# Three projections of a hybrid layer: plain fp32 matmuls in place of three fp32r products of split operands

## The chip, the cores and the metric

The kernel runs on one core of a Trainium2 chip. The metric is device time in microseconds (us) for one execution. Times inside an execution are us from the start of its span; the span is the time from its first to its last instruction. The engines are TensorE (PE: matmuls and transposes; PEld: its weight loads), VectorE (DVE), ScalarE (ACT), GpSimd (POOL) and SyncE (SP), whose queue issues most DMAs.

## The reference, cut to what matters

Two sequences of 128 tokens (context and latent, `NS = 2`) go through two layers (`DEPTH = 2`), all in fp32.

```
h = rmsnorm(x, norm_g) * (1 + scale) + shift           # (128, 1024); shift, scale, gate from adaLN of the condition
z = h @ w_in                                           # split into the parts below
conv_in (2*512), conv_gate (512), ssm_in (512), ssm_gate (512), q (512), k (128), v (128), attn_gate (512), merge (3*1024)
branch A: GLU of conv_in, depthwise convolution of 31 taps, layernorm, silu
branch B: state space scan over ssm_in in two directions, gelu, GLU
branch C: attention with 8 query and 2 key heads
x = x + gate * ((sum of sigmoid(merge) * branch @ w_branch) @ w_out)
```

`ssm_in` and the two halves of `conv_in` are the first three projections here: columns 1536 to 2047 (unit `ssm`), 0 to 511 (`ca`, the value half) and 512 to 1023 (`cg`, the gate half).

## The kernel before, in words

**Order.** `order(l)` writes out by hand the stages of a layer, and every engine walks the same list `todo`, doing its own part of each stage. In layer 0 it starts: `hT` (2), `early` (2), `chunks cg`, `unit cg`, `preE 0`, `preP 1`, `unit ssm`, `unit ca`, `pack`, `preE 1`, ... `UT`, `S`, ... , `scan`. In layer 1 the same without `preE` and `preP`, which were done in layer 0, and with the second half of the last adaLN product (`adaEnd`) ahead of `cg` and its transposes (`adaT`) after it. Ahead of layer 0's list stands `preP 0`. `preP` is a chain of products and sums on POOL (L1766): for half 0 two rounds of two products and a sum over 128x512 (`tB`, `bbar`), then two rounds of two products (`tA`, `tB`) and a sum (`pre`) over 128x1024. `preE` transposes `pre` on PE and ACT copies it out (L1124). `S` reads its result, and the scan on DVE reads `S`.

**Operands.** `hT` holds the normalised and modulated activations, transposed: per token set 8 tiles of 128x128. Weights arrive as slabs of 2 k-tiles by 512 columns (512 KB), into a ring of `RAW = 4` buffers (`raw`); SP waits for the read of the slab four before (`slab_read`) and issues the next (L663).

**A plain unit** (`plain_slab`, L753) multiplies `hT` with the raw slab: 8 k-tiles by 2 token sets, each an fp32 matmul of 128x128 by 128x512 into one PSUM bank a token set. `q`, `kv`, `sg`, `gg`, `ag` are such units. In the trace one such matmul appears as two instructions. Its slab is released when PE has read it.

**A split unit** (`split_unit`) uses fp32r operands in two parts. Of each k-tile of weights (a chunk) ACT writes the high part (`high_parts`, L1082, a copy to fp32r) and DVE the low part (`low_parts`, L1342, raw minus high); of `hT` the same is made once (stage `early`: ACT L1201, DVE `tt_` L1342, into `mixed_split` and `gates_split`). PE then does hi*hi (L1028), hi*lo (L1029) and lo*hi (L1030) for each k-tile and token set. The slab is released when the low part of its second k-tile is done, not when PE has multiplied. Parts lie in three rooms (`CHUNK_ROOMS`): for the units in `EARLY` these are two halves of `qM` and a piece of `gates`, else pieces of `wide` and `utok`. `ahead` lets ACT and DVE work two chunks beyond the end of the unit in hand, but not from an early unit to a late one.

`cg` waits for the low part of `hT` (`early_lo`). Behind `ssm` its result goes to `utok`, from there by 8 DMAs to `wide` (`pack_u`), ACT packs it (`pack`, L1213) and PE transposes it (`UT`), which opens the way to `S`. `tt_` is the helper of DVE (L1342) and of POOL (L1766).

Of the kernel before, what the change touches and what calls it, by code (L numbers as in the profile page):

```python
# [41 lines left out]
F32 = mybir.dt.float32  # L42
F32R = mybir.dt.float32r
ALU = mybir.AluOpType
ACT = mybir.ActivationFunctionType
# [3 lines left out]
NS = 2  # L49
D = 1024  # L50
DT = D // P
DEPTH = 2
W = 512
# [25 lines left out]
ADA_COLS = D // 4  # L79
ADA_ROWS = P // 4  # L80
MERGE_OF = {"A": 0, "B": 1, "C": 2}
EARLY = ("cg", "ssm", "ca")
CHUNK_ROOMS = 3

LAST_COMB = ("comb", BRANCHES[-1], 1)
# [5 lines left out]
def order(l):  # L91

    def nxt(*stage):
        return [stage] if l + 1 < DEPTH else []

    def last(*stage):
        return [] if l + 1 < DEPTH else [stage]

    n = l + 1
    return ([("hT", 0), ("hT", 1), ("early", 0), ("early", 1), ("chunks", "cg")]  # L100
            + ([("adaEnd", l, 2)] if l else []) + [("unit", "cg")] + ([("adaT", l, 2)] if l else [])
            + ([("preE", 0, 0), ("preP", 0, 1)] if l == 0 else [])
            + [("unit", "ssm"), ("unit", "ca"), ("pack",)] + ([("preE", 0, 1)] if l == 0 else [])
            + [("bz", 0), ("UT",), ("S",), ("cp",), ("convT", 0), ("convT", 1), ("scan", 0, 16, ()),
               ("unit", "q"), ("unit", "kv"), ("scan", 16, NCHUNK, (0, 1)),
               ("unit", "sg"), ("K", 0), ("bz", 1), ("qkn", 0), ("qkn", 1)]
            + [("unit", "gg"), ("K", 1), ("unit", "ag"), ("Y",), ("qkT", 0), ("qkT", 1), ("att", 0)]
            + nxt("small", n) + nxt("tab", n) + nxt("ada", n, 0) + nxt("adaT", n, 0)
            + [("gelu", 0), ("gelu", 1)] + nxt("ada", n, 1) + [("geT", 0), ("geT", 1)] + nxt("adaT", n, 1)
            + last("split", 0) + last("split", 1) + [("att", 1), ("unit", "glub"), ("unit", "glua")]  # L110
            + (nxt("split", 0) + nxt("split", 1) + nxt("conv", 10, 21, None))
            + ([("ada", 0, 2)] if l == 0 else []) + nxt("cT", n) + ([("adaT", 0, 2)] if l == 0 else [])
            + nxt("preP", n, 0) + [("chunks", "meB0"), ("brT", "B", 0), ("brT", "B", 1)]
            + nxt("conv", 21, 26, "B0") + last("conv", 10, 17, "B0") + [("comb", "B", 0)]
            + [("brT", "C", 0), ("brT", "C", 1)] + nxt("conv", 26, TAPS, "B1") + last("conv", 17, 24, "B1")
            + [("comb", "B", 1)] + nxt("taps", n)
            + nxt("preE", n, 0) + nxt("preP", n, 1) + last("conv", 24, TAPS, "C0")
            + [("comb", "C", 0), ("cback", 0), ("cback", 1), ("comb", "C", 1)] + nxt("preE", n, 1)
            + [("brT", "A", 0), ("brT", "A", 1), ("comb", "A", 0), ("comb", "A", 1)]
            + [("wout", 0), ("wout", 1)] + nxt("xn", n, 0) + nxt("xn", n, 1) + nxt("ada", n, 2))  # L120
# [25 lines left out]
def split_unit(u):  # L146


    return u[:2] in ("me", "br", "wo") or u in EARLY


def side_uses(l, stage):
# [83 lines left out]
def build(nc, A, C, O):  # L236

    with ExitStack() as ctx:
# [15 lines left out]
        def sem(name):  # L254
            if name not in sems:
                sems[name] = ctx.enter_context(nc.semaphore(name))
            return sems[name]
# [81 lines left out]

        late_room = [wides[:, 0:2 * W], wides[:, 2 * W:4 * W], utoks[:, 0:2 * W]]  # L340

        early_room = [qMs[:, 0:2 * W], qMs[:, 2 * W:4 * W], gatess[:, 4 * W:6 * W]]
        hTe = [room[:, 0:2 * D].rearrange("p (s t q) -> p s t q", s=NS, t=DT) for room in (mixeds, gatess)]
        kz = [sb("kz0", [P, KV, P]), sb("kz1", [P, KV, 2 * P])]

        prob, probT = (pre[:, r, :, :, :].rearrange("p g j c -> p (g j c)").rearrange("p (b k) -> p b k", b=2)
# [63 lines left out]
                chunk_read.append((proj.full, proj.at[(l, u, NS - 1)][0] + 1))  # L410

        def chunk_parts(m):
            room = (early_room if chunks[m][1] in EARLY else late_room)[m % CHUNK_ROOMS]
            return room[:, 0:W], room[:, W:2 * W]

        def chunk_raw(m):
# [3 lines left out]
        def ahead(l, u, beside=2):  # L420

            m = max(i for i, c in enumerate(chunks) if c[:2] == (l, u)) + 1
            room = 0 if m == len(chunks) or (chunks[m][1] in EARLY) != (u in EARLY) else beside
            return m + room


# [20 lines left out]

        split_hi = sem("split_hi")
        split_lo = sem("split_lo")
        early_lo = sem("early_lo")  # L450
        consts_in = sem("consts_in")
        expo_in = sem("expo_in")
        rope_in = sem("rope_in")
# [57 lines left out]
        def ls(l, s):  # L511

            return NS * l + s + 1
# [21 lines left out]

        parts = []
        for l, stg in todo:
            if stg[0] in ("early", "split", "brT"):
                parts.append((l,) + stg)
            elif stg in (LAST_COMB, ("wout", 0)):  # L540
                parts += [(l, "mixT", s, int(stg != LAST_COMB)) for s in range(NS)]
# [176 lines left out]
        def _(pe):  # L718
# [45 lines left out]
            for l, stg in todo:  # L764
# [228 lines left out]
                    m.then_inc(side.full, 1)  # L993
                if k in ("unit", "comb", "wout") and stg[1] not in ("glub", "glua"):
                    for u, nk, n in units_of(stg):
                        if u in EARLY:
                            if u == EARLY[0]:
                                pe.wait_ge(early_lo, ls(l, NS - 1))
                            lhs = hTe
                        elif u[:2] == "br":  # L1000
                            for s in range(NS):
                                side.drained(pe, ("brT", l, u[2], s))
                            lhs = brTs[u[2]]
                        elif u[:2] == "me":
                            pe.wait_ge(split_lo, ls(l, NS - 1))
                            lhs = hTs
                        else:
                            lhs = hT
# [43 lines left out]
        def _(act):  # L1052
# [19 lines left out]
            def high_parts(upto):  # L1072

                for m in range(highs[0], upto):
                    l_, u, kt = chunks[m]
                    slab_landed(act, (l_, u, kt // KT_SLAB))
                    if u == "me" + BRANCHES[0] + "0" and kt == 0:
                        act.wait_ge(y_in, 16 * 8 * (l_ + 1))
                        act.wait_ge(gelu_pre, NS * (l_ + 1))
                    if m >= CHUNK_ROOMS:  # L1080
                        act.wait_ge(*chunk_read[m - CHUNK_ROOMS])
                    S.activation(chunk_parts(m)[0], chunk_raw(m), ACT.Copy).then_inc(chunk_hi, 1)  # L1082
                    highs[0] = m + 1

            for l, stg in todo:
# [51 lines left out]
                elif k == "hT":  # L1137
# [5 lines left out]
                        m = S.activation(hT[:, s, i, :], side.bank(key)[:, P * i:P * i + P], ACT.Identity,  # L1143
                                         bias=ada[:, l, i, s:s + 1], scale=gsc[:, l, i, s:s + 1])
                    m.then_inc(side.freed(key), 1)
                elif k == "unit" and stg[1] == "ca":
                    high_parts(ahead(l, "ca"))
                elif k == "unit" and stg[1] == "kv":
                    if l:
                        act.wait_ge(out_done, 64 * l)  # L1150
# [4 lines left out]
                        S.activation(v[:, s, :], proj.bank(key)[:, P:2 * P], ACT.Copy).then_inc(proj.freed(key), 1)  # L1155
                elif k == "unit" and stg[1] in ("ssm", "q"):
                    if stg[1] == "ssm":
                        high_parts(ahead(l, "ssm"))
                        if l:
                            act.wait_ge(gelu_done, NS * l)  # L1160
                    for s in range(NS):
# [6 lines left out]
                            src = src.rearrange("p (a h d) -> p a h d", a=2, h=4)  # L1168
                        S.activation(dst, src, ACT.Copy).then_inc(proj.freed(key), 1)
                elif k == "unit" and stg[1] in ("cg", "glub"):  # L1170
                    if stg[1] == "cg":
                        high_parts(ahead(l, "cg"))
                    for s in range(NS):
                        key = (l, stg[1], s)
                        proj.filled(act, key)
# [18 lines left out]
                    high_parts(ahead(l, "br" + unit, CHUNK_ROOMS))  # L1194
                elif k == "chunks":
                    high_parts(chunk_at[(l, stg[1], 0)] + CHUNK_ROOMS)
                elif k == "early":
                    s = stg[1]
                    side.drained(act, ("hT", l, s, 0))
                    side.drained(act, ("hT", l, s, 1))  # L1200
                    S.activation(hTe[0][:, s, :, :], hT[:, s, :, :], ACT.Copy).then_inc(split_hi, 1)  # L1201
                elif k == "split":
                    s = stg[1]
                    if s == 0:
# [125 lines left out]
        def _(dve):  # L1330
# [10 lines left out]
            def tt_(out, a, b, op=ALU.mult):  # L1341
                return V.tensor_tensor(out, a, b, op)  # L1342


            def low_parts(upto):

                for m in range(lows[0], upto):
                    hi, lo = chunk_parts(m)
                    dve.wait_ge(chunk_hi, m + 1)
                    tt_(lo, chunk_raw(m), hi.bitcast(F32), ALU.subtract).then_inc(chunk_lo, 1)  # L1350
                    lows[0] = m + 1
# [61 lines left out]
            for l, stg in todo:  # L1413
# [111 lines left out]
                                            gsc[:, l, d, s:s + 1], ada[:, l, d, s:s + 1], ALU.mult, ALU.add)  # L1525
                    m.then_inc(side.freed(key), 1)
                elif k == "unit" and stg[1] == "ca":
                    low_parts(ahead(l, "ca"))
                    for s in range(NS):
                        key, ka = (l, "cg", s), (l, "ca", s)  # L1530
                        proj.filled(dve, ka)
                        th_ready(dve, key)
                        V.scalar_tensor_tensor(y2[:, s, :], th_view(key), 1.0, proj.bank(ka)[:, :],
                                               ALU.add, ALU.mult).then_inc(proj.freed(ka), 1)
                elif k == "unit" and stg[1] in ("cg", "ssm"):
                    low_parts(ahead(l, stg[1]))
                elif k == "unit" and stg[1] == "glua":
                    for s in range(NS):
                        key = (l, "glua", s)
# [178 lines left out]
                                link(m)  # L1718
                elif k == "chunks":
                    low_parts(chunk_at[(l, stg[1], 0)] + CHUNK_ROOMS)  # L1720
                elif k == "early":
                    s = stg[1]
                    dve.wait_ge(split_hi, part_at[(l,) + stg] + 1)
                    tt_(hTe[1][:, s, :, :], hT[:, s, :, :], hTe[0][:, s, :, :].bitcast(F32),
                        ALU.subtract).then_inc(early_lo, 1)
                elif k == "split":
                    s = stg[1]
                    dve.wait_ge(split_hi, part_at[(l,) + stg] + 1)
# [172 lines left out]
```

## Time and profile before

| what | value |
|---|---|
| median of 3 runs | 833.03 us (832.92 to 834.3) |
| profiled execution | 833.01 us, span 831.2 us |
| mean granted TensorE clock | 0.902 |
| PE busy | 669.3 us, 81% |
| DVE busy | 605.6 us, 73% |
| ACT busy | 313.0 us, 38% |
| POOL busy | 173.8 us, 21% |

Busy time is the time in which an engine had at least one instruction running. Matmuls overlap one another, so their mean duration is longer than the distance from one to the next. Layer 0's three early units run from 51 to 99 us, those of layer 1 from 482 to 518 us.

### The profile page before, as it was taken

The page shows a single profiled execution, that of the slowest core. Times are in us where ns is not written, and L with a number is a line of the kernel's source. Part 1 is how long each engine was busy: PE and PEld are TensorE (multiplying, and loading weights), DVE is VectorE, ACT ScalarE, POOL GpSimd, SP SyncE. Part 2 cuts the span into 40 slices and gives each one's busy share as a digit, 9 for nine tenths or more (in the row PEclk, how much of TensorE's full clock was granted, in tenths as well). Part 3 has the DMA queues.
Part 4 walks back from the last instruction along what each step waited for, and adds up shares of the span by engine and source line. Part 5 has one row for each costly group of instructions (what it writes and reads, how often), then busy time and mean ns, then how long its engine had stood idle before and what let it go on. Part 6 is the DMA issues. An engine that isn't in the chain of part 4 may idle for free.

```text
span 831.2 us, 9693 instructions
## 1 busy us (share of the span) xinstructions
PE 669.3 (81%) x3450; PEld 466.9 (56%) x3450; DVE 605.6 (73%) x1103; ACT 313.0 (38%) x557; POOL 173.8 (21%) x121
## 2 busy tenths in 40 slices
PE   3757899980848964989999889999807689999996
PEld 1245765540723543866877567655407347777785
DVE  3388599997355699777767545999974567988664
ACT  1344541211423221544654445411114524545552
POOL 1088269102000046061000200591020000000000
PEclk9579999995876967999999989999958898999999
DMA  6953526350078462545554565354220124655651
GB/s 250 264 158 105 189 72 187 108 148 7 5 177 283 126 229 59 173 125 152 175 177 153 180 222 171 109 178 125 67 85 11 38 78 138 184 165 167 186 180 53
DMA packets 79339, 117.66 MB, mean 142 GB/s; under 512 B 27436, under 2 KB 31868, under 8 KB 79292
## 3 DMA queue, kind: packets, MB, share of 16 engines
q1 hardware_dynamic: 78460, 116.52, 46.1%
q10 hardware_dynamic: 832, 0.53, 0.3%
q8 instruction: 27, 0.44, 0.2%
q14 instruction: 20, 0.16, 0.1%
HBM read 112.51 MB, written 1.38 MB: 137 GB/s over the span
## 4 chain that ended last, share of the span: by engine, by line
PE 45%; DVE 37%; DMA 5%; POOL 4%; SPq 3%; ACT 3%; issue 2%; DVEq 0%; ACTq 0%; POOLq 0%
PE proj L1028 11%; PE proj L1030 11%; PE proj L1029 11%; DVE cvacc L1407 9%; DVE H L1342 8%; DVE qkt L1342 7%; DMA raw<-in_w_ada 4%; PE side L762 4%; PE proj L753 3%; PE side L959 2%; DVE wide_split L1342 2%; DVE H L1562 2%; SPq L611 1%; POOL tB L1766 1%; DVE qM_split L1342 1%
## 5 line engine op out<-in xcount | busy, mean ns | idle before, releaser
L753 PE MATMUL proj<-raw,hT 128*128 128x512 f32 (+1 forms) x320 | 125.1, 551 | 0.0
L1407 DVE SCALAR_TENSOR_TENSOR cvacc<-cvpad,taps,cvacc 128x256 f32<-128x256 f32 x240 | 122.9, 540 | 0.0
L1342 DVE TENSOR_TENSOR wide_split<-raw,wide_split 128x512 fp32r<-128x512 f32 x118 | 90.8, 774 | 40.1 <-ACT wide_split L1082 39.1
L1082 ACT ACTIVATE wide_split<-raw 128x512 fp32r<-128x512 f32 x118 | 74.6, 633 | 95.6 <-PE proj L1030 95.6
L753 PEld LDWEIGHTS proj<-raw,hT 128*128 128x128 f32 x320 | 60.3, 190 | 60.4 <-issue 58.4
L1342 DVE TENSOR_TENSOR H<-H,qkt 128x128 f32<-128x128 f32 x128 | 75.4, 589 | 1.2
L1028 PE MATMUL proj<-wide_split,H_split 128*128 128x512 f32 x154 | 64.7, 420 | 14.1 <-DVE wide_split L1342 13.6
L1770 POOL TENSOR_SCALAR st<-st 128x1 f32<-128x1 f32 (+1 forms) x12 | 3.9, 326 | 331.3 <-DVE st L1679 146.9
L730 PE MATMUL proj<-raw,cond 128*32 128x256 f32 x384 | 43.6, 561 | 26.7 <-DMA raw<-in_w_ada 26.6
L957 PE MATMUL side<-qM,Uz 128*64 128x64 f32 x128 | 19.8, 241 | 54.4 <-DVE HY L1663 54.4
L1030 PE MATMUL proj<-wide_split,H_split 128*128 128x512 f32 x154 | 62.3, 404 | 0.0
L1029 PE MATMUL proj<-wide_split,H_split 128*128 128x512 f32 x154 | 62.3, 404 | 0.0
L1342 DVE TENSOR_TENSOR utok_split<-raw,utok_split 128x512 fp32r<-128x512 f32 x58 | 45.4, 783 | 18.4 <-ACT utok_split L1082 17.4
L1082 ACT ACTIVATE utok_split<-raw 128x512 fp32r<-128x512 f32 x58 | 36.7, 632 | 42.9 <-PE proj L1030 42.9
L1342 DVE TENSOR_TENSOR qM_split<-raw,qM_split 128x512 fp32r<-128x512 f32 x32 | 37.0, 1167 | 19.7 <-ACT qM_split L1082 19.6
L957 PEld LDWEIGHTS side<-qM,Uz 128*64 128x64 f32 x128 | 14.2, 155 | 56.0 <-issue 56.0
L1028 PEld LDWEIGHTS proj<-wide_split,H_split 128*128 128x128 f32 x154 | 29.9, 194 | 26.9 <-DVE wide_split L1342 18.0
L730 PEld LDWEIGHTS proj<-raw,cond 128*32 128x32 f32 x384 | 10.1, 133 | 55.4 <-DMA raw<-in_w_ada 51.8
L1028 PE MATMUL proj<-qM_split,mixed_split 128*128 128x512 f32 x64 | 27.6, 432 | 15.7 <-DVE qM_split L1342 15.7
L1342 DVE TENSOR_TENSOR qkt<-H,lamI 128x128 f32<-128x128 f32 x64 | 37.3, 582 | 1.4
L1182 ACT ACTIVATE gates<-proj 128x512 f32<-128x512 f32 x12 | 7.1, 597 | 75.9 <-PE proj L753 62.6
L1766 POOL TENSOR_TENSOR tA<-cT,lamr 128x1024 f32<-128x1024 f32 (+1 forms) x12 | 19.7, 1642 | 74.4 <-PE side L863 73.6
(235 smaller groups left out, 1496.2 us busy)
## 6 DMA issues: line engine op xcount, KB each, us to landing
raw<-in_w_in SPq DMA_DIRECT2D x104, 512.0 KB, 3.7
raw<-in_w_ada SPq DMA_DIRECT2D x48, 512.0 KB, 5.2
raw<-in_w_out SPq DMA_DIRECT2D x16, 512.0 KB, 3.9
raw<-in_w_ssm_glu SPq DMA_DIRECT2D x8, 512.0 KB, 5.7
raw<-in_w_ssm_out SPq DMA_DIRECT2D x8, 512.0 KB, 3.8
raw<-in_w_attn_out SPq DMA_DIRECT2D x8, 512.0 KB, 4.0
raw<-in_w_conv_out SPq DMA_DIRECT2D x8, 512.0 KB, 4.0
raw<-in_w_in SPq DMA_DIRECT2D x8, 256.0 KB, 2.7
```

The costliest lines, as they stand in the source:

```text
L730: m = T.matmul(proj.bank(stg)[ADA_ROWS * j:ADA_ROWS * j + ADA_ROWS, 0:ADA_COLS], cond[:, kt, :], w[:, 0, ADA_COLS * j:ADA_COLS * j + ADA_C ...
L753: m = T.matmul(proj.bank((l, u, s))[:, 0:n], lhs[:, s, kt, :], w[:, i, :], start=(kt == 0), stop=last)
L762: return T.transpose(out, in_, ident[0:k, 0:k])
L957: T.matmul(o, Uz[:, g, :], M[:, :, g // 2, :], start=True, stop=False)
L959: m = T.matmul(o, HY[:, q % 2, gi, r, :, :].rearrange("p s k -> p (s k)"), CP[:, r, 1:L + 1, g, :], start=False, stop=(r == 1))
L1028: T.matmul(bank[:, :], hi, whi, start=(kt == 0), stop=False)
L1029: T.matmul(bank[:, :], hi, wlo, start=False, stop=False)
L1030: m = T.matmul(bank[:, :], lo, whi, start=False, stop=last)
L1082: S.activation(chunk_parts(m)[0], chunk_raw(m), ACT.Copy).then_inc(chunk_hi, 1)
L1342: return V.tensor_tensor(out, a, b, op)
L1407: m = V.scalar_tensor_tensor(acc, src, taps[:, t, j:j + 1], acc, ALU.mult, ALU.add)
L1766: return Q.tensor_tensor(out, a, b, op)
```

## The change

`EARLY` is gone: `cg`, `ssm` and `ca` are no longer split units. PE multiplies `hT` with the raw slabs in `plain_slab`, as it does for `q` or `gg`. The stages `early` (the split of `hT`) and `chunks cg` (the first three chunks) leave the order, and so do the calls of `high_parts` and `low_parts` in these three units, the early rooms and the semaphore `early_lo`. In place of `early_lo`, PE waits ahead of `cg` until both halves of `hT` are written for both token sets. `ahead` stops at the end of a layer, where it used to stop at the edge between early and late units. Slabs of the three units are now released by PE's reads.

```diff
@@ order
-    return ([("hT", 0), ("hT", 1), ("early", 0), ("early", 1), ("chunks", "cg")]
+    return ([("hT", 0), ("hT", 1)]
@@ split_unit
-    return u[:2] in ("me", "br", "wo") or u in EARLY
+    return u[:2] in ("me", "br", "wo")
@@ chunk_parts, ahead
-            room = (early_room if chunks[m][1] in EARLY else late_room)[m % CHUNK_ROOMS]
+            room = late_room[m % CHUNK_ROOMS]
...
-            room = 0 if m == len(chunks) or (chunks[m][1] in EARLY) != (u in EARLY) else beside
+            room = 0 if m == len(chunks) or chunks[m][0] != l else beside
@@ tensor engine
-                        if u in EARLY:
-                            if u == EARLY[0]:
-                                pe.wait_ge(early_lo, ls(l, NS - 1))
-                            lhs = hTe
-                        elif u[:2] == "br":
+                        if u == "cg":
+                            for s in range(NS):
+                                for h in range(2):
+                                    side.drained(pe, ("hT", l, s, h))
+                        if u[:2] == "br":
@@ scalar engine
-                elif k == "unit" and stg[1] == "ca":
-                    high_parts(ahead(l, "ca"))
...
-                        high_parts(ahead(l, "ssm"))
...
-                        high_parts(ahead(l, "cg"))
...
-                elif k == "early":
-                    s = stg[1]
-                    side.drained(act, ("hT", l, s, 0))
-                    side.drained(act, ("hT", l, s, 1))
-                    S.activation(hTe[0][:, s, :, :], hT[:, s, :, :], ACT.Copy).then_inc(split_hi, 1)
@@ vector engine
-                    low_parts(ahead(l, "ca"))
...
-                elif k == "unit" and stg[1] in ("cg", "ssm"):
-                    low_parts(ahead(l, stg[1]))
...
-                elif k == "early":
-                    s = stg[1]
-                    dve.wait_ge(split_hi, part_at[(l,) + stg] + 1)
-                    tt_(hTe[1][:, s, :, :], hT[:, s, :, :], hTe[0][:, s, :, :].bitcast(F32),
-                        ALU.subtract).then_inc(early_lo, 1)
```

## Rows read from the trace of the kernel before

**Rows 1.** The page's busy time, share of the span and instructions of each engine.
```profile
PE 669.3 (81%) x3450; PEld 466.9 (56%) x3450; DVE 605.6 (73%) x1103; ACT 313.0 (38%) x557; POOL 173.8 (21%) x121
```

**Rows 2.** Chain of waits, layer 0: start us, us, what.
```profile
66.16 2.72 POOL pre L1766
...
83.80 2.80 DVE qM_split L1342
...
99.38 2.43 PE side L762 x24
```

**Rows 3.** Chain of waits, layer 1.
```profile
476.40 3.77 DMA raw<-in_w_in
...
480.85 0.70 DVE qM_split L1342
...
513.98 0.23 PE proj L1028
...
517.90 0.24 PE proj L1030
```

**Rows 4.** Instructions in order, layer 0: start, us, engine, line, what [idle before <-releaser].
```profile
40.77 3.53 SPq L663 DMA_DIRECT2D raw<-in_w_in  x4
...
44.24 1.36 DVE L1524 TENSOR_SCALAR hT<-side,gsc,ada 128x128 f32<-128x128 f32 x4 [0.21 <-PE side L762]
...
51.05 0.77 PE L1028 MATMUL proj<-qM_split,mixed_split 128*128 128x512 f32 x1 [6.85 <-DVE qM_split L1342]
...
70.68 0.48 PE L1028 MATMUL proj<-gates_split,mixed_split 128*128 128x512 f32 x1
...
78.97 0.50 PE L1028 MATMUL proj<-qM_split,mixed_split 128*128 128x512 f32 x1 [1.11 <-DVE qM_split L1342]
```

**Rows 5.** Instructions in order, PE alone, layer 1: the unit `gg` and what follows it.
```profile
567.51 14.00 PE L753 MATMUL proj<-raw,hT 128*128 128x512 f32 x32
581.44 4.63 PE L876 MATMUL side<-EC,bz 128*48 128x80 f32 x64
```

**Rows 6.** DMA issues from 40.5 to 41.3 us: count, KB each, us to landing.
```profile
raw<-in_w_in SPq DMA_DIRECT2D x1, 512.0 KB, 5.4
```

**Rows 7.** Stretches, PE alone: us, busy us (instructions), granted clock, DMA share, GB/s.
```profile
51.00:53.50 2.50, 2.45 (x6) 0.50 0.03 3
...
66.00:99.30 33.30, 27.45 (x119) 1.00 0.39 121
...
481.70:487.00 5.30, 5.30 (x13) 0.50 0.67 236
...
627.20:630.80 3.60, 3.60 (x34) 0.50 0.00 0
```

**Rows 8.** Instructions in order, layer 1.
```profile
475.37 1.37 DVE L1524 TENSOR_SCALAR hT<-side,gsc,ada 128x128 f32<-128x128 f32 x4 [0.57 <-PE side L762]
...
481.69 0.76 PE L1028 MATMUL proj<-qM_split,mixed_split 128*128 128x512 f32 x1 [3.53 <-DVE qM_split L1342]
...
514.62 1.90 ACT L1213 ACTIVATE HY<-wide 64x2048 f32<-64x2048 f32 x1
...
518.06 1.14 PE L762 MATMUL side<-ident,HY 64*128 64x64 f32 x15
```

**Rows 9.** Instructions in order, POOL alone.
```profile
43.93 2.19 POOL L1766 TENSOR_TENSOR tB<-ss,tA 128x512 f32<-128x512 f32 x2 [15.83 <-DMA tA<-in_ssm_b_im]
...
61.28 2.36 POOL L1766 TENSOR_TENSOR tA<-lamr,bbar 128x1024 f32<-128x1024 f32 x1
...
71.08 2.05 POOL L1766 TENSOR_TENSOR tA<-lamr,bbar 128x1024 f32<-128x1024 f32 x1 [2.20 <-PE side L762]
...
117.35 1.93 POOL L1766 TENSOR_TENSOR tA<-cT,lamr 128x1024 f32<-128x1024 f32 x1
...
311.04 1.34 POOL L1766 TENSOR_TENSOR bbar<-tB 128x512 f32<-128x512 f32 x1
...
324.15 2.42 POOL L1766 TENSOR_TENSOR pre<-tA,tB 128x1024 f32<-128x1024 f32 x1
```

More of the change, by code:

```diff
@@ L81 @@
 MERGE_OF = {"A": 0, "B": 1, "C": 2}
-EARLY = ("cg", "ssm", "ca")
 CHUNK_ROOMS = 3
@@ L340, in build @@
         late_room = [wides[:, 0:2 * W], wides[:, 2 * W:4 * W], utoks[:, 0:2 * W]]
-        early_room = [qMs[:, 0:2 * W], qMs[:, 2 * W:4 * W], gatess[:, 4 * W:6 * W]]
-        hTe = [room[:, 0:2 * D].rearrange("p (s t q) -> p s t q", s=NS, t=DT) for room in (mixeds, gatess)]
         kz = [sb("kz0", [P, KV, P]), sb("kz1", [P, KV, 2 * P])]
@@ L449, in build @@
         split_lo = sem("split_lo")
-        early_lo = sem("early_lo")
         consts_in = sem("consts_in")
@@ L537, in build @@
         for l, stg in todo:
-            if stg[0] in ("early", "split", "brT"):
+            if stg[0] in ("split", "brT"):
                 parts.append((l,) + stg)
@@ L1170, in _ @@
                 elif k == "unit" and stg[1] in ("cg", "glub"):
-                    if stg[1] == "cg":
-                        high_parts(ahead(l, "cg"))
                     for s in range(NS):
```

## The prediction
> **What bounds the kernel now.** I read the busy shares first [rows 1]: TensorE (PE) is at 81% and VectorE (DVE) at 73%, so neither alone sets the time. Then I read the chain of waits in the two stretches that the change touches, one in each layer.
>
> In layer 0 [rows 2] the chain is not the matmuls. It runs on GpSimd (POOL) up to the last `pre` product of `preP`, which ends at 68.9, goes through the four banks of transposes of `preE` half 0, and then sits on the low parts that DVE makes of the raw slabs, up to 2.8 us each where layer 1 needs 0.70 [rows 3]. PE runs the `ssm` unit from 70.68 [rows 4], and the transposes that open the rest of the layer start at 99.38, when `ca` is through. Everything after that hangs on it in series: transposes, `S`, and the scan on DVE.
>
> In layer 1 [rows 3] nothing runs on POOL at that time. The chain waits for the first slab of `w_in` (3.77 us from 476.40, there at 480.17), passes one copy and one subtraction, and from 481.69 to the `UT` transposes at 518.06 [rows 8] it is matmul after matmul: PE is the bound, for 36.4 us. The mean of the profiled matmuls (0.40 us) is no price here, since they overlap; the distance from one to the next is: 17 steps from 513.98 to 517.90, 0.231 us each [rows 3].
>
> The time: the profiled execution took 833.01 us around a span of 831.2; the median of the runs shown is 833.03. The sum below is a difference to the execution, and carries over as it is.
>
> **What the change does to PE.** Each layer has three such units of 8 k-tiles by 2 token sets. Now each pair costs three fp32r matmuls, 3 x 0.231 = 0.69 us; a unit is 48 matmuls, 11.1 us. Afterwards it is one plain fp32 product, which the trace holds as two instructions. The later unit `gg` has that very shape: it took from 567.51 to 581.44, 13.93 us, with the clock at full rate and no gap [rows 5]. So each unit costs PE 2.8 us more where PE is what is waited for, and it is so in layer 1 throughout, in layer 0 only where DVE held it at less than that.
>
> Removed with it, per layer: 24 copies on ScalarE (ACT, 0.63 us), 24 subtractions on DVE, and the split of `hT`, two instructions on either. What of it shows in the end is worked out below by stage: in layer 1 the copy and subtraction ahead of the first matmul (1.5 us), in layer 0 what it did to POOL. The rest lies beside PE's matmuls and gives nothing. Nothing is added on any queue. Slabs are now released by PE's last read, no more by the low parts which ran ahead; a slab feeds PE for 3.5 us (13.93 / 4), three others are in hand (10.4 us), and a slab took 3.8 to 5.4 us from issue to landing [rows 3, 6], so I cost this at nothing. `gg` lives on the same release and shows no gap.
>
> **Layer 1.** PE starts when the slab is there, 480.2, in place of 481.69: 1.5 us gained (`hT` is finished before, at 476.7 [rows 8]). Then 3 x 13.93 = 41.8, and the small transposes between `cg` and `ssm`, 0.2, which is what is left of the 36.4 when 144 x 0.231 = 33.3 and the clock's 2.9 are taken off. The clock has to be added. Here the granted clock had fallen to half during the wait and stayed there until about 487.5, 5.8 us long, which lost 2.9; after the start of `cg` in layer 0 it was low for only 2.9 us, from 51.05 to 54.0, which lost 1.5 [rows 7]. PE's idle time before the new start is 2.0 us, not 3.5. I take 2.2, the middle of these, with 0 and 2.9 as bounds. The end: 480.2 + 41.8 + 0.2 + 2.2 = 524.4, against 518.06: **+6.3 us** (+4.1 to +7.0). The packing of `u`, which `UT` needs too, ended at 516.5, 1.5 us ahead of those transposes [rows 8]; it counts from the end of `ssm`, and the `ca` unit that lies over it grows by 2.8, so it does not come last.
>
> **Layer 0.** Four steps.
> First, `cg` can start when `hT` is drained (45.6) and the first slab has landed, 40.77 + 5.4 = 46.2 [rows 4, 6], in place of 51.05. With 13.9 and 1.5 to 2.9 of low clock it ends at 61.6 to 63.0. That gives nothing: PE then waits for `pre` from POOL.
> Second, POOL itself. While DVE subtracts, the two alternate: a 128x1024 product of `preP` takes 2.36, a sum 2.72 [rows 2, 9]. Where DVE was idle at its start a product took 2.05, and a sum took 2.42 beside a tap of the convolution; a 128x512 sum took 1.34 in layer 1's `preP`, and two 128x512 products 2.19 with the 0.07 between them, 1.06 each [rows 9]. After the change DVE is idle from 45.6 until `ca`. With 0.07 us between instructions: 43.93 + 2 x (1.13 + 1.13 + 1.41) + 2 x (2.12 + 2.12 + 2.49) = 64.8 in place of 68.9: **-4.1 us**. The bounds are nothing and that.
> Third, the `preE` transposes as before, 1.8 from the end of `pre` (68.88) to `ssm` (70.68) [rows 2, 4]: `ssm` starts at 66.6.
> Fourth, `ssm` and `ca`: 27.9 instead of 28.7 (70.68 to 99.38, much of it DVE's pace): -0.8. So the end is 94.5 at full clock, 4.9 earlier.
> Against it stands the clock. Before, PE waited in this stretch too, but no more than 1.1 us at a time (before 78.97), and the granted clock stayed at 1.00 [rows 4, 7]. Now PE idles 1.8 to 3.2 us ahead of the transposes. After its idle stretches of 6.85 us (before 51.05) and 3.53 us (before 481.69) the clock was low [rows 4, 8]. I take 1.5, bounds 0 and 2.9. Layer 0: **-3.4 us** (-4.9 to -2.0).
>
> The Trainium skill, page "SBUF — State Buffer", section "Who interferes with whom", says that a DVE instruction with two SBUF inputs and a GpSimd instruction that reads SBUF exclude each other for a whole instruction. By that rule all of POOL's excess (2.36 against 2.05) goes away; the rows above give the same 4.1, and without the rule the bound of nothing would weigh more.
> The skill's page "TensorE: Matmul & The Clock Gate", section "HAM oscillation — how this bites in real kernels", says that a tensor engine kept idle between bursts drops to half clock and starts each burst cold. By it the new gap in layer 0 costs a whole low spell and not my compromise of 1.5; the rival (b) prices that from rows.
>
> Sum: -3.4 + 6.3 = +2.9; 833.0 + 2.9 = **835.9 us**. Behind either stretch the work is a chain to the end of the layer, so I let both differences pass through unchanged.
>
> **Rivals.**
> (a) As forecast: 835.9, own range 834.7 to 837.4. Chance 0.50.
> (b) The clock falls at both starts and stays low for the long spell seen in layer 1: -2.0 + 7.0 = +5.0, 838.0. For it: both long waits before had that effect. Against: the gaps are shorter. 0.20.
> (c) POOL isn't faster alone, `pre` still ends at 68.9. PE has then idled some 6 us, the clock is low for certain: 27.9 + 2.9 against 28.7 gives +2.1, with +6.3 it is +8.4, 841.4. For it: I infer the alternation from durations, and in the scan stage POOL's products take 1.93 beside a busy DVE [rows 9], as if it cost POOL nothing. Against: the 2.05 of [rows 9] beside the 2.36. 0.10.
> (d) The other side. The price of layer 1 is certain, so a gain could come from the clock alone: full at both starts, -4.9 + 4.1 = -0.8, 832.2; and if the burst of `Y` matmuls, 3.6 us at half rate before [rows 7], also starts warm, 1.8 more: 830.4. It counts as faster only when more than 4.6 of the 5.5 us at stake (1.5 + 2.2 + 1.8) is saved. 0.05 for that, 0.10 for the part that ends between 832.2 and 834.
> (e) PE waits for slabs after all, since they are requested later. The nearest row is the 3.77 us of the first slab in layer 1 [rows 3]; one such wait more in each layer gives +2.9 + 7.6 = +10.5, 843.5. 0.05.
>
> A measurement of this kernel tells about 0.2%, 1.7 us, from no change: 831.4 to 834.7 counts as the same. Slower: (a), (b), (c), (e) = 0.85; same 0.10; faster 0.05. The range from 832.4 to 841.0 leaves out (c), (e) and the faster part of (d), less than 0.2.
>
> **What would show it.** In the profile after: 32 matmuls of 13.9 us in each of the six units; in layer 0 a PE start near 46, idle time near 62, `pre` done near 64.8 with products of 2.05, and the block of transposes before `UT` near 96 (99.4 before); in layer 1 a start 1.5 us earlier relative to the adaLN matmuls, and about 44 us from there to `UT`. The prediction is wrong if `pre` ends near 68.9, if the granted clock differs by more than 3 us of low spell from what I took, if slabs are waited for inside a unit, or if the differences don't reach the end.

## The result and the profile after

The changed kernel takes 836.11 us, the median of 9 runs (834.4 to 839.15), beside 832.73 for the kernel before on the same chips (9 runs, 831.33 to 834.3). The ratio is 1.0035, 95% interval 1.0022 to 1.0049, which is 2.9 us slower (1.8 to 4.1); the two medians differ by 3.4. The profiled execution took 836.93, 0.8 over the median, around a span of 835.1: 3.9 more than the 831.2 before. The lines below explain the 3.9.

The page, busy time of the engines, answering to [rows 1]:

```profile
PE 689.5 (83%) x3354; PEld 453.9 (54%) x3354; DVE 543.6 (65%) x1051; ACT 280.2 (34%) x505; POOL 168.6 (20%) x121
```

DVE is relieved of 62 us and the kernel is slower all the same: nearly all of that work lay beside something else. PE has 20 us more.

**Layer 0.** The chain of waits (start us, us, what), answering to [rows 2]:

```profile
62.00 2.35 POOL pre L1744
...
64.39 3.49 PE side L758 x16
67.89 27.61 PE proj L749 x64
95.50 2.43 PE side L758 x24
...
99.42 1.14 PE side L859 x8
```

The low parts are gone from it. Between POOL's last sum and the transposes that open the rest of the layer there are only PE's own blocks. They start at 95.50, 3.9 us earlier than before (99.38).

Instructions in order, POOL and then PE, answering to [rows 4, 9]:

```profile
43.96 2.19 POOL L1744 TENSOR_TENSOR tB<-ss,tA 128x512 f32<-128x512 f32 x2 [15.78 <-DMA tA<-in_ssm_b_im]
46.23 1.27 POOL L1744 TENSOR_TENSOR bbar<-tB 128x512 f32<-128x512 f32 x1
...
57.80 2.02 POOL L1744 TENSOR_TENSOR tA<-lamr,bbar 128x1024 f32<-128x1024 f32 x1
...
62.00 2.34 POOL L1744 TENSOR_TENSOR pre<-tA,tB 128x1024 f32<-128x1024 f32 x1
```
```profile
46.32 15.67 PE L749 MATMUL proj<-raw,hT 128*128 128x512 f32 x32 [1.95 <-DMA raw<-in_w_in]
64.39 3.49 PE L758 MATMUL side<-ident,pre 128*128 128x128 f32 x16 [2.40 <-POOL pre L1744]
67.68 27.81 PE L749 MATMUL proj<-raw,hT 128*128 128x512 f32 x64
```

POOL starts where it did. Its first two products take 2.19 us as before; from the first sum on (46.23) every instruction of its chain is shorter, and `pre` is done at 64.34, where it was 68.88. PE is through with `cg` at about 62.0, waits 2.40 us, and then takes 3.3 us (64.39 to 67.68) for the 16 transposes that took 1.8 before. The stretches, PE alone (us, busy us, granted clock), say why, and answer to [rows 7]:

```profile
62.00:64.00 2.00, 0.00 (x0) 1.00 0.36 60
64.80:67.80 3.00, 3.00 (x16) 0.50 0.10 34
68.50:95.00 26.50, 26.50 (x63) 1.00 0.48 143
...
475.50:477.50 2.00, 0.45 (x1) 1.00 1.04 397
478.00:481.00 3.00, 3.00 (x5) 0.50 0.85 307
481.50:520.00 38.50, 38.50 (x93) 1.00 0.59 172
```

The clock is still full in the idle time and at half (1.2 GHz) just when PE has work again: it falls at about 64.7 and 477.7, 0.3 and 0.6 us after PE has begun, and is back at 68.1 and 481.1. It was at half at the start of `cg` in layer 0 too, from 47.5 to 50.9, behind the wait of 1.95 us; that is why `cg` took 15.67 us there, where it takes 13.97 at full clock (in the kernel with added subtractions, below).

**Layer 1.** The chain of waits, answering to [rows 3, 8]:

```profile
472.12 1.06 PE proj L726 x8
...
473.20 3.71 DMA raw<-in_w_in
476.91 0.14 issue
477.05 15.67 PE proj L749 x32
492.71 0.22 PE side L758 x2
...
522.56 1.14 PE side L859 x8
```

From the last adaLN block to the first matmul of `S` it was 475.32 to 520.29, 44.97 us; now it is 472.12 to 522.56, 50.44. That is +5.5.

The rest: 372.7 us from the first matmul of `S` in layer 0 to the adaLN block (372.0 before), and 312.5 from `S` of layer 1 to the end (310.9). So -3.9 + 0.7 + 5.5 + 1.6 = +3.9. The two stretches that the change touches give +1.6 of it, the two whose code is the same +2.3.

### The profile page after: what moved, and what is told of

It is laid out like the page before. It is cut to its first block, busy times and chain, and to the rows that moved or that the text cites. A ratio compares the mean times of both kernels' runs of the same rounds, so it can differ in the third digit from the quotient of the medians.

```text
span 835.1 us, 9347 instructions
## 1 busy us (share of the span) xinstructions
PE 689.5 (83%) x3354; PEld 453.9 (54%) x3354; DVE 543.6 (65%) x1051; ACT 280.2 (34%) x505; POOL 168.6 (20%) x121
## 4 chain that ended last, share of the span: by engine, by line
PE 48%; DVE 35%; DMA 5%; POOL 4%; SPq 3%; ACT 2%; issue 2%; DVEq 0%; ACTq 0%; POOLq 0%
PE proj L749 11%; PE proj L1024 9%; PE proj L1025 9%; PE proj L1026 9%; DVE cvacc L1393 9%; DVE H L1328 8%; DVE qkt L1328 7%; DMA raw<-in_w_ada 4%; PE side L758 4%; PE side L955 2%; DVE wide_split L1328 2%; DVE H L1545 2%; SPq L607 1%; PE side L953 1%; DVE qk L1328 1%
## 5 line engine op out<-in xcount | busy, mean ns | idle before, releaser
L749 PE MATMUL proj<-raw,hT 128*128 128x512 f32 (+1 forms) x512 | 211.9, 574 | 4.0 <-DMA raw<-in_w_in 4.0
L749 PEld LDWEIGHTS proj<-raw,hT 128*128 128x128 f32 x512 | 97.9, 193 | 111.4 <-issue 107.1
L1393 DVE SCALAR_TENSOR_TENSOR cvacc<-cvpad,taps,cvacc 128x256 f32<-128x256 f32 x240 | 119.5, 525 | 0.0
L1328 DVE TENSOR_TENSOR H<-H,qkt 128x128 f32<-128x128 f32 x128 | 73.6, 575 | 1.2
L1518 DVE SCALAR_TENSOR_TENSOR mixed<-th,proj 128x512 f32<-128x512 f32 x4 | 2.8, 688 | 75.7 <-PE proj L749 75.7
L1024 PEld LDWEIGHTS proj<-wide_split,H_split 128*128 128x128 f32 x154 | 30.2, 196 | 27.8 <-DVE wide_split L1328 17.2
L1026 PEld LDWEIGHTS proj<-wide_split,H_split 128*128 128x128 f32 x154 | 30.3, 196 | 7.3
L1025 PEld LDWEIGHTS proj<-wide_split,H_split 128*128 128x128 f32 x154 | 30.4, 197 | 5.8
```

Source lines behind the costliest of these rows:

```text
L749: m = T.matmul(proj.bank((l, u, s))[:, 0:n], lhs[:, s, kt, :], w[:, i, :], start=(kt == 0), stop=last)
L1024: T.matmul(bank[:, :], hi, whi, start=(kt == 0), stop=False)
L1025: T.matmul(bank[:, :], hi, wlo, start=False, stop=False)
L1026: m = T.matmul(bank[:, :], lo, whi, start=False, stop=last)
L1393: m = V.scalar_tensor_tensor(acc, src, taps[:, t, j:j + 1], acc, ALU.mult, ALU.add)
```

## The experiments

Unless said otherwise each kernel was timed in 5 rounds against the kernel before. Ratios are turned into us with 833.

### Each layer by itself

`EARLY` became a list of pairs of layer and unit, so that the units of one layer are split and those of the other plain. The first list leaves layer 0 plain, the second layer 1.

```diff
-    return u[:2] in ("me", "br", "wo") or u in EARLY
+    return u[:2] in ("me", "br", "wo") or (l, u) in EARLY_AT
...
+EARLY_AT = ((1, 'cg'), (1, 'ssm'), (1, 'ca'))
...
+EARLY_AT = ((0, 'cg'), (0, 'ssm'), (0, 'ca'))
```

> Plain fp32 units in layer 0 alone; layer 1 keeps the split ones. Theory (the change is a gain in layer 0, because POOL's chain is no longer slowed by DVE, and a loss in layer 1, because PE needs 13.9 instead of 11.1 us a unit): 3 to 4 us faster than before, near 829.3, with the transposes before UT of layer 0 near 95.5 as in the profile of the change. Rival (layer 0's earlier end is lost again behind it, and the whole +3.4 stems from some common cost): within 1 us of before.

Measured: 828.73 us, ratio 0.9935 (0.9912 to 0.9959): 5.4 us faster than before (3.4 to 7.3).

> Plain fp32 units in layer 1 alone; layer 0 keeps the split ones. Theory: 5.5 to 7 us slower than before, near 839, from the start of the first unit to UT about 43.3 us in place of 36.4. Rival (both layers carry half of the +3.4): 1.5 to 2 us slower. The differences of this kernel and of the one with layer 0 alone should add up to the +3.4 of the whole change within 1 us.

Measured: 841.22 us, ratio 1.0078 (1.0053 to 1.0102): 6.5 us slower (4.4 to 8.5). In its profile the stretch from the adaLN block to `S` is 50.36 us (476.18 to 526.54), that of the change to 0.1 us. The profile of this kernel also shows how far an untouched stretch can move: with the same split units as before in layer 0, `S` of layer 0 starts at 105.38, 2.1 us later than before (103.30).

What follows: the change is a gain and a loss. Both rivals fall, no common cost and no equal halves. The sum of the two is +1.1, the whole change +2.9; they differ by 1.8, more than the 1 us that I allowed, but each of the two ratios is only known to about 2 us. By the medians (833.4 for the kernel before in these rounds) the two are -4.7 and +7.8, +3.1 in sum beside the +3.4 of the whole change, within what I allowed; the runs don't tell more exactly. In the profile of the first kernel the transposes before `UT` start at 93.64:

```profile
46.21 16.96 PE L756 MATMUL proj<-raw,hT 128*128 128x512 f32 x32 [1.89 <-DMA raw<-in_w_in]
64.33 2.00 PE L765 MATMUL side<-ident,pre 128*128 128x128 f32 x16 [1.17 <-POOL pre L1779]
66.17 27.63 PE L756 MATMUL proj<-raw,hT 128*128 128x512 f32 x64
93.64 1.94 PE L765 MATMUL side<-ident,pre 128*128 128x128 f32 x16
```

That is 1.7 earlier than in the change (95.33 in the same view), with the same work. Here `cg` took 16.96 and left PE only 1.17 us to wait, and the transposes ran at full clock. Whether executions of one kernel differ in this way isn't shown, since each has one profile.

### One unit alone

```diff
+EARLY_AT = ((0, 'cg'), (0, 'ssm'), (0, 'ca'), (1, 'cg'), (1, 'ssm'))
```

> Only the last of the three units of layer 1 (ca) as plain fp32, all else as before. Theory (13.93 - 11.1 a unit, nothing at the start): 2.8 us slower, near 835.5; the unit itself 13.9 us. Rival (the loss of layer 1 is in its first unit, the clock and the start, not in the rate): less than 1 us slower.

Measured: 837.88 us (12 runs, 833.33 to 839.13), ratio 1.0035 (1.0017 to 1.0054): 2.9 us slower (1.4 to 4.5). The medians differ by 4.5, since the 12 runs lie wide apart. The chain of waits in its layer 1:

```profile
508.48 0.23 PE proj L1038
508.71 13.75 PE proj L756 x32
```

The unit took 13.75 us where 48 split matmuls take 11.1. From the adaLN block to `S` it was 47.58 us (477.03 to 524.61), 2.6 more than before (44.97). The loss is the rate, 2.7 us a unit, as the theory had it; the rival falls.

### What slowed POOL

Twelve instructions on DVE in the changed kernel, where it is otherwise idle:

```diff
+                    if l == 0 and s == 1:
+                        for i in range(12):
+                            link(tt_(gates[:, i % 2, 0, :], x[:, 0, 0:W], x[:, 1, 0:W], ALU.subtract))
```

> The changed kernel with 12 DVE instructions added right after hT of layer 0: subtractions of two 128x512 fp32 halves of x in SBUF, into a tile that is overwritten later. They do nothing for the result and no one waits for them. Theory (two SBUF operands on DVE slow POOL): preP's 128x1024 products go back from 2.02 to about 2.36 and the sums from 2.34 to 2.7, pre ends near 68 in place of 64.3, and the kernel is 3 to 4.5 us slower than the change, near 840. Rival (POOL was slowed by ACT's copies or the loads, not by DVE): pre still ends near 64.4 and the time is that of the change, 836.1.

Measured: 840.68 us, ratio 1.0089 (1.0074 to 1.0103). Against the change, 1.0089 - 1.0035 = 0.54%, 4.5 us slower. DVE, then POOL, in order:

```profile
45.12 23.37 DVE L1328 TENSOR_TENSOR gates<-x 128x512 f32<-128x512 f32 x12
```
```profile
59.69 2.35 POOL L1747 TENSOR_TENSOR tA<-lamr,bbar 128x1024 f32<-128x1024 f32 x1
...
64.55 2.67 POOL L1747 TENSOR_TENSOR pre<-tA,tB 128x1024 f32<-128x1024 f32 x1
```

The counterpart, DVE as busy with one operand in SBUF:

```diff
+                        for i in range(30):
+                            link(V.tensor_reduce(st[:, 140:141], x[:, 0, 0:W], AX_X, ALU.add))
```

> The changed kernel with 30 DVE instructions added at the same place: sums along a row of a 128x512 fp32 half of x, one operand in SBUF, one column out, never used. DVE is about as long busy as with the 12 subtractions. Theory (only a second SBUF operand of DVE stands in POOL's way): products of 2.02, pre ends near 64.4, time as the change, 836.1. Rival (any busy DVE slows POOL): pre ends near 68 and 3 to 4.5 us slower than the change.

Measured: 837.24 us, ratio 1.0043 (1.0029 to 1.0058). The intervals of this and of the change overlap. DVE, then POOL:

```profile
46.47 21.58 DVE L1515 TENSOR_REDUCE st<-x 128x1 f32<-128x512 f32 x30
```
```profile
45.02 2.19 POOL L1747 TENSOR_TENSOR tB<-ss,tA 128x512 f32<-128x512 f32 x2 [16.86 <-DMA tA<-in_ssm_b_im]
...
58.90 2.02 POOL L1747 TENSOR_TENSOR tA<-lamr,bbar 128x1024 f32<-128x1024 f32 x1
...
63.10 2.35 POOL L1747 TENSOR_TENSOR pre<-tA,tB 128x1024 f32<-128x1024 f32 x1
```

POOL's chain up to the end of `pre` took 24.9 us before (43.93 to 68.88), 20.4 in the change, 23.7 with the subtractions, 20.4 with the sums (45.02 to 65.45; it started a microsecond later because its operand landed later). So it is this DVE work that holds POOL up, and not any busy DVE; ACT's copies and the loads aren't needed for it. The subtractions bring back 3.3 of the 4.5 us. The rest stands beside work that they don't imitate: before, DVE split `hT` with two subtractions of 128x1024 (46.01 to 49.45) and went on to the first chunks, and beside this POOL's first sum took 2.16 in place of 1.27 and its next two products 3.38 in place of 2.19.

The two loads differ in one thing more than the number of operands from SBUF: a subtraction writes 512 columns, a row sum one. No run separates the two. What the profile of the change has on it: four DVE instructions that write 128x128 to SBUF from a PSUM operand (`hT`, 44.41 to 45.78) lie beside POOL's first products, and these took 2.19, as the next two did with DVE idle.

It holds in both directions: the 12 subtractions took 23.4 us in all, where one takes 0.70 alone [rows 3]. POOL lost 3.3 us to subtractions that would take 8.4 by themselves (an estimate, 12 x 0.70), so the two engines still overlapped for a part of each.

### What the idle time does to the clock

```diff
+                    if ll == 0 and half == 0:
+                        for i in range(2):
+                            T.matmul(long_banks[0][:, :], hT[:, 0, i, :], x[:, 0, 0:W], start=True, stop=True)
                     pe.wait_ge(pre_done, 2 * ll + half + 1)
```

> The changed kernel with two fp32 matmuls of 128x128 by 128x512 added on PE in layer 0 between cg and the transposes of preE half 0, into a PSUM bank that is not read; 1.75 us of work in the idle 2.4 us. Theory (the idle time brought the clock down to half and made the block of transposes 3.49 us where it was 1.8): clock full through the block, ssm starts near 66.1 in place of 67.7, and the kernel is 1.5 to 2 us faster than the change, near 834.4. Rival (the transposes are slow for another reason, such as ACT's copies of each bank): no difference.

Measured: 834.81 us (12 runs, 830.74 to 839.04), ratio 1.0017 (1.0000 to 1.0033); against the change 0.18%, 1.5 us faster, in size as the theory has it, but the intervals overlap. The profile is plainer, PE alone in order and then the stretches:

```profile
61.81 1.88 PE L811 MATMUL long<-x,hT 128*128 128x512 f32 x4
64.44 2.00 PE L758 MATMUL side<-ident,pre 128*128 128x128 f32 x16 [0.75 <-POOL pre L1747]
66.28 27.63 PE L749 MATMUL proj<-raw,hT 128*128 128x512 f32 x64
```
```profile
64.50:66.20 1.70, 1.70 (x16) 1.00 0.31 121
```

With 0.75 us of waiting left the clock stays full, the transposes take 1.8 us again, and `ssm` starts at 66.28 in place of 67.68. ACT's copies of the banks are the same in both, so the rival falls in this profile: the block is slow when the clock is at half. That the filling kept the clock up is not shown by it. In the kernel with the row sums PE waited longer than in the change, at the same place, and the clock stayed full too (1.00 from 65.5 to 67.3):

```profile
65.50 2.00 PE L758 MATMUL side<-ident,pre 128*128 128x128 f32 x16 [2.49 <-POOL pre L1747]
```

### The part that gains, without its idle time

In layer 0, `ssm` ahead of `preE` half 0, and layer 1 split as before:

```diff
-            + ([("preE", 0, 0), ("preP", 0, 1)] if l == 0 else [])
-            + [("unit", "ssm"), ("unit", "ca"), ("pack",)]
+            + [("unit", "ssm")]
+            + ([("preE", 0, 0), ("preP", 0, 1)] if l == 0 else [])
+            + [("unit", "ca"), ("pack",)]
```

> As the kernel with layer 0 alone, and in layer 0 PE and ACT take the unit ssm ahead of the transposes of preE half 0, so that PE has work while POOL still makes pre. Theory: PE runs from 46.3 without a gap, 15.6 + 13.9 + 1.8 + 13.9, so the transposes before UT come near 91.5 in place of 95.3: 3 to 4 us more than the kernel with layer 0 alone, 7 us faster than before in all, near 825.5. Rival (POOL's second half, which now starts 8 to 10 us later, ends after ca and takes the gap's place): no faster than with layer 0 alone.

Measured: 824.05 us (820.32 to 826.08), ratio 0.9877 (0.9850 to 0.9903): 10.3 us faster than before (8.1 to 12.5). The profiled execution is the 820.32, the fastest of the six. PE alone:

```profile
46.22 27.70 PE L757 MATMUL proj<-raw,hT 128*128 128x512 f32 x64 [1.67 <-DMA raw<-in_w_in]
73.76 2.00 PE L766 MATMUL side<-ident,pre 128*128 128x128 f32 x16
75.59 13.90 PE L757 MATMUL proj<-raw,hT 128*128 128x512 f32 x32
89.33 1.95 PE L766 MATMUL side<-ident,pre 128*128 128x128 f32 x16
```

PE has no gap from 46.22 on, and this time no low clock either. The block before `UT` starts at 89.33, 6.0 before that of the change (95.33) and 4.3 before that of the kernel with layer 0 alone (93.64). In these two profiles some 3 of the 4.3 is the clock of `cg` (16.96 there, 13.8 here), which the new order doesn't touch: the kernel below has a low spell in `cg` again, 29.40 us for the two units. The medians, 4.7 us apart, with intervals that don't overlap, are the better measure of the order. POOL's second half ended at 89.1, just in time: the rival comes within 0.3 us of being true, so moving more work ahead should gain nothing, which no run tests.

The same with three matmuls of `x` on PE behind `adaEnd` of layer 1:

```diff
                         ada_slab(("ada",) + stg[1:], kt)
+                    if k == "adaEnd":
+                        for i in range(3):
+                            T.matmul(long_banks[0][:, :], x[:, 0, P * i:P * i + P], x[:, 1, 0:W], start=True, stop=True)
```

> The kernel with layer 0 alone, reordered, and in layer 1 (split units) three fp32 matmuls of 128x128 by 128x512 of x added on PE behind the last adaLN matmuls, where PE waits 3.5 us for the first slab of w_in; their result goes to a PSUM bank and is not read. Theory (that wait is what brings the clock down, and 2.9 us were lost to it): the granted clock stays full at the start of cg, from the last adaLN matmuls to UT 40 in place of 42.8 us, and 2 to 3 us faster than without the added matmuls, near 821.5. Rival (the clock falls there whatever PE does, or the added matmuls delay cg by what they save): no faster, 824.

Measured: 822.05 us, ratio 0.9854 (0.9839 to 0.9868), the fastest of all, by 2 us, though its interval overlaps that of the kernel above. In the profile PE waits 0.80 us at the start of `cg`, the clock is full from there, and the adaLN block to `S` takes 42.35 us (468.78 to 511.13) where the kernel without the added matmuls has 43.78 and the kernel before 44.97. `S` of layer 1 comes 1.4 us sooner behind the adaLN block, where 2 to 3 were expected. The total is not settled. For the low spell one more fact speaks: all eight profiles in which PE waited 2.0 us or more ahead of `cg` of layer 1 (2.01 to 3.53) have a low spell within its first microsecond, and the two with less (0.80 here, 1.39 in the kernel with the gap filled) have none.

## Why the prediction was right

Forecast 835.9, measured 836.11. The way was the one described: POOL freed and an earlier end in layer 0, the rate of PE in layer 1. That the number is met to 0.2 us is luck. In the profile the two stretches gave +1.6 where I had +2.9, and what made up for it, and more, came from parts that I had put at nothing. Term by term, against the profile of the change:

| term | forecast | profile |
|---|---|---|
| POOL's `pre` done | 64.8 (-4.1) | 64.34 (-4.5) |
| low clock at the gap of layer 0 | +1.5 | +1.5 |
| transposes before `UT`, layer 0 | -3.4 | -3.9 |
| start of PE in layer 1 | -1.5 | -1.4 |
| a plain unit at full clock | 13.93 | 13.78 (27.56 for two, from 492.77) |
| low clock in layer 1 | 2.2 | 1.7 |
| layer 1 in all | +6.3 | +5.5 |
| passed on unchanged | 0 | +0.7 and +1.6 |
| sum | +2.9 | +3.9 |

The step that the rows could not show, that POOL gets faster when DVE is idle, was right, and that DVE's subtractions are its cause is shown by the pair of added loads. Uncontended instructions were a little shorter than my nearest rows: 2.02 and 2.34 where I took 2.05 and 2.42, 1.26 where I took 1.34.

The clock term of layer 0 was a middle between two bounds and its exactness is luck. In the change the gap of 2.40 us cost 3.3 - 1.8 = 1.5 us; in the kernel with layer 0 alone the gap was 1.17 us and cost nothing, and in the one with DVE's row sums it was 2.49 us and cost nothing either: its transposes took 2.00 with their overlap, as before. In the kernel with the subtractions PE waited 7.39 us, and the clock was at half from 64.9 to 71.7. In layer 1 the low spell was 3.4 us (477.7 to 481.1) and lost 1.7; in the kernel with the gap filled the wait there was 1.39 us in place of 2.01, there was no low spell, and `cg` of layer 1 took 13.97, not 15.67.

"I let both differences pass through unchanged" was not quite true: 2.3 us were added behind the two stretches in this execution. 0.8 of it lies here: the matmuls of `Y` in layer 1, from their start to the `q` transposes behind them, took 13.2 us before (627.2 to 640.4) and 14.0 after (629.4 to 643.4), and the granted clock, low since long before the burst in both, was at half up to 630.9 before and up to 634.7 after. A stretch of the change, PE alone:

```profile
630.00:634.00 4.00, 4.00 (x40) 0.50 0.02 4
```

The same work in the reordered kernel took 12.8 us, with the clock at half only up to 618.1, 2.8 us into it. Another 1.4 lies in the attention behind it: from the transposes of `qk` to those of `mixed` it was 14.4 us before (640.41 to 654.83), at full clock up to 651.3, and 15.9 after (643.36 to 659.22), with the clock at half from 648.3 to 651.7. Some 0.5 comes back behind that. Between the ten profiles of this study, with no difference in the code of these parts, the time from `S` of layer 1 to the end lies between 310.1 and 313.2 us, and that from `S` of layer 0 to the adaLN block between 370.8 and 373.7. The +1.6 and the +0.7 are within this spread, so these profiles can't say whether the change causes them.

Rival (b) named this mechanism and overrated it: both low spells came, 3.4 us long each. The section that the prediction names for it, "HAM oscillation — how this bites in real kernels" of the Trainium skill's page "TensorE: Matmul & The Clock Gate", tells of waits of 3 to 5 us between bursts. The gap here was 2.40 us, so the page by itself did not carry the whole low spell that I read out of it; what spoke for (b) were the rows. (c), a POOL that stays slow, fell. The row that it leaned on, a product of 1.93 beside a busy DVE, stands in the change as well (113.47): there DVE paid, two `H<-H,qkt` of 128x128 took 4.44 us from 117.68, where one takes 0.28 at its shortest. (d), a gain from the clock alone, did not come: the lowest of the nine runs is 834.40. The range that I gave leaves out (c), (e) and the faster part of (d), and their chances add up to 0.20, not to less. (e), slabs asked for later, fell: all six units ran without a wait for a slab.

## What to carry to other kernels

Giving one engine less work helps only where it is waited for. The same edit gained 4 to 5 us in the layer where DVE and POOL held each other up and lost 5.5 to 6.5 (7.8 by the medians) in the layer where PE alone was the bound, and taking it where it gains, with the order changed so that PE isn't left idle, gave -1.2% in place of +0.35%. Ask of each stage by itself who is waited for, and price a change by the distance between starts there, not by busy time. Where the chain runs over POOL, look at what DVE does beside it, and how many operands it takes from SBUF.

## What the runs showed that I had not expected

A DVE subtraction of 128x512 fp32 from SBUF, 0.70 us alone, took 1.95 us each beside POOL's instructions (12 in 23.4), and POOL's products 2.35 in place of 2.02; 30 row sums on DVE, busy for 21.6 us, left POOL at 2.02.

Idle times of PE as short as 1.89 us are followed by a low spell, and the length of the wait alone doesn't decide it. At the gap of layer 0 one of 2.40 us was, those of 0.75 and 1.17 us were not, but neither was one of 2.49. At the start of `cg` in layer 0 five profiles with waits of 1.89 to 2.20 us have a low spell (in the change from 47.5 to 50.9), and two with 1.67 and 2.11 have none. The fall came at times during the wait and at times up to 1.2 us after PE had begun to work again (0.6 in layer 1 of the change). Single runs of one kernel lie up to 8 us apart (830.74 to 839.04 with the gap filled). That these spells are the cause isn't shown: the mean granted clock of those two runs is 0.903 and 0.909, the faster run having the lower. Effects under 2 us showed themselves only in the profile, and one profile of each kernel doesn't settle them.
